# The start of a two-block transformer stack in split float32: another order of loads, splits, squares and norm sums in the first stage

## The chip, the cores and the metric

The kernel runs on one core of one Trainium2 chip. A core has a matmul engine (TensorE, PE in the profile), VectorE (DVE), ScalarE (ACT), GpSimd (POOL) and SyncE (SP), which issues most DMAs. Each engine works through its own instructions in order, and semaphores tie them together. The metric is the device time of one execution in microseconds (us); less is better.

## The reference, cut to what matters

Two blocks run one after the other on a sequence of 256 tokens plus 16 meta tokens, 272 columns in all, with 1024 features. Each block has two layers. A layer of the first block is a feed-forward part (ffn), a mixer and a second ffn:

```python
for l in range(DEPTH):
    h = h + 0.5 * swiglu(rms_norm(h, ffn1_norm[l]), ffn1_w_gu[l], ffn1_w_down[l])
    u = rms_norm(h, mix_norm[l])
    ...
    h = h + merged @ w_out[l]
    h = h + 0.5 * swiglu(rms_norm(h, ffn2_norm[l]), ffn2_w_gu[l], ffn2_w_down[l])
```

`rms_norm(h, w)` is h times w, divided by the root of the mean of h squared over the features; `swiglu` is silu(x W_gate) times x W_up, times W_down. The second block also adds a table of relative-position bias (`rel_bias`) to its attention scores. All of it is float32.

## The kernel before

The activations h lie transposed, as 8 tiles (k = 0 to 7) of 128 features by 272 tokens. A product of the matmul engine takes operands that were rounded, so every float32 operand is split in two: a high part, made by ScalarE (`x_hi` for h times the gain, L868; `split_hi` for weights, L858), and a low part, the rest, made by VectorE (`x_lo`, L1212; `split_lo`, L1201). Each product is then three matmuls: low weight by high input, high weight by low input, high by high. A weight chunk `raw[k]` holds the 8 feature tiles (1024 columns) that make one output tile; four chunks stand in a ring and are called a quad.

The first ffn of the first layer is the stage that the change is about. Its quad 0 is `raw[0]` to `raw[3]`. The first two output tiles (0 and 1) run as a group in `first_tiles` (L546 to L548): for every feature tile i, the three matmuls of chunk 0 and then those of chunk 1, 48 matmuls in all. Then come tiles 2 to 7, one by one, 24 matmuls each, in `k8_tile` (L513 to L515), and then a loop over quads. Tile 4 is the first one of quad 1, tile 8 the first one of quad 2.

The division by the root is put off. GpSimd squares the 8 tiles of h and adds them up in `acc` (one squaring, then seven pairs of a squaring L1795 and an addition L1798), TensorE sums `acc` over the features with a matrix of ones (`norm_sum`, L522), ScalarE takes the root (`std`, L862), VectorE the reciprocal (`rstd`, L1206), and VectorE multiplies each finished tile by it as it reads it out (`z`). In this stage the sum stands on TensorE between tiles 1 and 2. On ScalarE and VectorE the splits of quad 1 stand ahead of the root and the reciprocal (`first_splits`); each may start when the tile that used its place in the ring is done.

Before the stage the program does some small things: SyncE loads the one-hot bucket rows and the bias table (semaphore `rel_in`), the vectors with all gains (`vec`), h in two halves, four weight chunks, the constants and the masks. TensorE makes the bias rows with one product (`brow`, L827), ScalarE copies them (L1150), SyncE writes them to memory (`rows`). VectorE works out two small coefficient vectors (`lb`, `lam`, L1642 to L1684) in 24 instructions on 4 or 8 columns, with ScalarE's Exp and Ln between them (L1162 to L1167), and casts the masks (L1686). These stand behind the splits of quad 0 and ahead of those of quad 1, on both engines. The order on every engine is the order in which the code is written.

Of the kernel before, what the change touches and what calls it, by code (L numbers as in the profile page):

```python
# [43 lines left out]
RING = 4  # L44
# [178 lines left out]
def program(nc, a):  # L223
    with ExitStack() as ctx:
# [106 lines left out]
        NORM = 7  # L331
# [105 lines left out]
        def _(sp):  # L437
            def load(src, q, k, cols):

                if not isinstance(q, int) or q >= 1:  # L440
                    sp.wait_ge(lo_made, (q - 1) * RING + k + 1)
                sp.dma_start(raw[:, k, 0:cols], src).then_inc(landed[k], 16)
# [8 lines left out]
                stream(a["ffn_gu"], f * 2 * KF, q, FFN_GU_QUADS, CH8)  # L451
                stream(a["ffn_down"], f * 2 * KD, q + FFN_GU_QUADS, FFN_DOWN_QUADS, CH11)

            sp.dma_start(onehot[0:N_BUCKETS + 1, :], a["bucket_rows"]).then_inc(rel_in, 16)
            sp.dma_start(relt[0:N_BUCKETS + 1, :], a["rel_rows"]).then_inc(rel_in, 16)
            sp.dma_start(vec[:, :], a["vectors"]).then_inc(vec_in, 16)
            for s in range(2):
                sp.dma_start(h[:, 4 * s:4 * s + 4, :], a["h0"][:, 4 * s:4 * s + 4, :]).then_inc(h_in[s], 16)
            for k in range(2):
                load(a["ffn_gu"][k], 0, k, CH8)  # L460
            sp.dma_start(consts[:, :], a["consts"]).then_inc(consts_in, 16)
            for k in range(2, RING):
                load(a["ffn_gu"][k], 0, k, CH8)
            sp.dma_start(gate_flat, a["masks"]).then_inc(masks_in, 16)
            sp.wait_ge(brow_made, 1)
            sp.dma_start(rows[:, :], brow[0:HEADS, :]).then_inc(rows_out, 16)
            stream(a["ffn_gu"], RING, 1, FFN_GU_QUADS - 1, CH8)
            stream(a["ffn_down"], 0, FFN_GU_QUADS, FFN_DOWN_QUADS, CH11)
            sp.wait_ge(rows_out, 16)
            stream(a["mix"], 0, FFN_QUADS, MIX_QUADS - HEADS, CH8)  # L470
# [34 lines left out]
        def _(pe):  # L505
# [32 lines left out]
            def first_tiles(q, group, src, c, ready, norm=None):  # L538


                hi, lo = src
                at_c = c if t_wide(hi) else 0

                def products(k, i):
                    out, w = bank[k][:, 0:T - c], slice(i * P, i * P + P)
                    pe.matmul(out, wlo[:, k, w], hi[:, i, at_c:], start=(i == 0), stop=False)  # L546
                    pe.matmul(out, whi[:, k, w], lo[:, i, at_c:], start=False, stop=False)  # L547
                    return pe.matmul(out, whi[:, k, w], hi[:, i, at_c:], start=False, stop=(i == 7))  # L548

                for k in range(group):  # L550
                    pe.wait_ge(lo_made, q * RING + k + 1)
                for i in range(6):
                    ready(i)
                    for k in range(group):
                        products(k, i)
                for k in range(group):
                    for i in (6, 7):
                        if k == 0:
                            ready(i)
                        mm = products(k, i)  # L560
                    mm.then_inc(tile_done, 1)
                    if norm and k == (0 if group == RING else group - 1):
                        norm()
# [12 lines left out]

            def ffn(q, j, x, n, f, c, main_norm=True):
                group = RING if c else 2
                first_tiles(q, group, (xhi, xlo), c, inputs_ready(x), input_norm(x, n, c) if main_norm else None)
                for t in range(group, 2 * RING):  # L580
                    k8_tile(q + t // RING, t % RING, j + 4 if t == 7 else None, early_bank(t), (xhi, xlo), c)
                with pe.Fori(2, FFN_GU_QUADS) as b:
                    for k in range(RING):
                        k8_tile(b + q, k, b * RING + j + k - 3, k, (xhi, xlo), c)
# [234 lines left out]
            def scores2(hd):  # L819
                if hd >= 2:  # L820
# [3 lines left out]
                          stop=True).then_inc(s2_done, 1)  # L824

            pe.wait_ge(rel_in, 32)
            pe.matmul(bank[6][0:HEADS, :], relt[0:N_BUCKETS + 1, :], onehot[0:N_BUCKETS + 1, :],  # L827
                      start=True, stop=True).then_inc(brow_done, 1)
            pe.wait_ge(consts_in, 16)
            pe.wait_ge(brow_made, 1)  # L830
            with pe.Fori(0, DEPTH) as l:
                ffn(**layer_stage(l, 0))
# [19 lines left out]
        def _(act):  # L852
# [263 lines left out]
            def attention():  # L1116
# [29 lines left out]
                norm_std(n + 1, c)  # L1146
                inputs_from_h(13, 12, c)

            act.wait_ge(brow_done, 1)
            act.activation(brow[0:HEADS, :], bank[6][0:HEADS, :], ACT.Copy).then_inc(brow_made, 1)  # L1150
            act.wait_ge(vec_in, 16)
            for k in range(KD):
                if k % 4 == 0:
                    act.wait_ge(h_in[k // 4], 16)
                x_hi(0, k, 0)
            for k in range(RING):
                split_hi(0, k, CH8, 0)
            act.wait_ge(consts_in, 16)
            act.activation(warm[:, :], eps, ACT.Copy)
# [37 lines left out]
        def _(dve):  # L1197
# [437 lines left out]
            for k in range(KD):  # L1635
                if k % 4 == 0:
                    dve.wait_ge(h_in[k // 4], 16)
                x_lo(0, k, 0)
            for k in range(RING):
                split_lo(0, k, CH8)  # L1640
            r0, r1 = vec[:, VEC["lb_raw"]:VEC["lb_raw"] + 4], vec[:, VEC["lb_raw"] + 4:VEC["lb_raw"] + 8]
            dve.tensor_tensor(lb[:, 3, 0:4], r0, r1, ALU.max)  # L1642
# [79 lines left out]
        def _(pool):  # L1722
# [66 lines left out]
            def of_layer(st):  # L1789
                squares_of(h, 0, st["n"] + 1, lambda k: pool.wait_ge(tile_read, st["j"] + 2 * KF + k + 1))  # L1790

            for k in range(KD):
                if k % 4 == 0:
                    pool.wait_ge(h_in[k // 4], 16)
                pool.tensor_tensor((sqt[:, k % 2, :] if k else acc[:, :]), h[:, k, :], h[:, k, :], ALU.mult)  # L1795
                pool.drain()
                if k:
                    op = pool.tensor_tensor(acc[:, :], acc[:, :], sqt[:, k % 2, :], ALU.add)  # L1798
# [124 lines left out]
```

## Time and profile before

| | us |
|---|---|
| median of 3 runs | 2566.45 |
| lowest and highest | 2561.85 and 2567.02 |
| the profiled execution | 2565.33 |
| its span | 2563.5 |
| TensorE busy | 2357.3 (92%) |
| VectorE busy | 1553.2 (61%) |
| ScalarE busy | 1146.8 (45%) |
| GpSimd busy | 693.1 (27%) |

The span runs from the first instruction to the last, and the profiled execution has 1.8 us outside it. TensorE is busy nearly everywhere, so a stretch in which it waits costs its length, and work on another engine costs nothing as long as TensorE doesn't come to wait for it. The mean clock that TensorE was granted is 0.952 of full speed.

### The profile page before, as it was taken

To read this page: it belongs to the slowest core of one execution; us is meant where nothing else is said; L and a number is where in the kernel's file an instruction comes from. 1 tells how busy PE (TensorE), PEld (TensorE's weight loads), DVE (VectorE), ACT (ScalarE), POOL (GpSimd) and SP (SyncE) were. 2 spreads that over 40 slices of the span, in tenths; PEclk is the share of its full clock that TensorE was granted. 3 is DMA by queue.
4 is the path that set the end of the run, shared out by engine and by line. 5 is a ranking of instruction groups with operands and counts; after the bars stand their busy time and mean duration, and the time that the engine had idled before them with its cause. 6 is when DMAs were issued, how large, how long until landed. Compare 5 with 4: busy or idle time off the path is not lost.

```text
span 2563.5 us, 50134 instructions
## 1 busy us (share of the span) xinstructions
PE 2357.3 (92%) x18052; PEld 2269.9 (89%) x18052; DVE 1553.2 (61%) x2043; ACT 1146.8 (45%) x1620; POOL 693.1 (27%) x737
## 2 busy tenths in 40 slices
PE   7999988899999999879999999976899899977997
PEld 7999875799999998856899999976799899966997
DVE  6556775465545557853655575587665755575654
ACT  5445542344444446432454345355453445343542
POOL 4321220133213211300332142234532222224321
PEclk9999997999999999887999999988899999988999
DMA  5554331255545544221455445533355455531552
GB/s 205 180 177 160 107 120 66 75 167 182 180 133 189 185 146 137 99 83 41 139 174 197 140 164 194 175 115 115 134 191 193 151 185 188 182 107 66 197 193 102
DMA packets 99326, 380.12 MB, mean 148 GB/s; under 512 B 10975, under 2 KB 13151, under 8 KB 99208
## 3 DMA queue, kind: packets, MB, share of 16 engines
q1 hardware_dynamic: 99208, 378.56, 43.6%
q8 instruction: 72, 1.18, 0.2%
q14 instruction: 46, 0.38, 0.0%
HBM read 377.46 MB, written 3.16 MB: 148 GB/s over the span
## 4 chain that ended last, share of the span: by engine, by line
PE 52%; issue 32%; POOL 6%; DVE 5%; POOLq 2%; ACT 2%; DVEq 1%; DMA 0%; ACTq 0%; SPq 0%
PE bank L513 16%; PE bank L515 16%; PE bank L514 16%; POOL acc L1731 2%; POOL kd L1777 2%; POOLq L1729 2%; PE bank L546 1%; PE bank L547 1%; PE bank L548 1%; DVE h L1503 1%; DVE wlo L1201 1%; DVE xlo L1212 1%; DVE rstd L1206 1%; POOL midlo L1785 1%; ACT whi L858 1%
## 5 line engine op out<-in xcount | busy, mean ns | idle before, releaser
L1201 DVE TENSOR_TENSOR wlo<-raw,whi 128x1024 fp32r<-128x1024 f32 (+1 forms) x660 | 897.3, 1370 | 418.3 <-ACT whi L858 417.3
L858 ACT ACTIVATE whi<-raw 128x1024 fp32r<-128x1024 f32 (+1 forms) x660 | 727.7, 1116 | 627.9 <-PE bank L515 586.2
L513 PE MATMUL bank<-xhi,wlo 128*128 128x272 f32 (+1 forms) x3344 | 967.5, 289 | 5.9 <-DVE wlo L1201 3.4
L515 PE MATMUL bank<-xhi,whi 128*128 128x272 f32 (+1 forms) x3344 | 962.5, 288 | 0.0
L514 PE MATMUL bank<-xlo,whi 128*128 128x272 f32 (+1 forms) x3344 | 960.5, 287 | 0.0
L513 PEld LDWEIGHTS bank<-xhi,wlo 128*128 128x128 f32 x3344 | 638.1, 191 | 8.6 <-issue 4.8
L515 PEld LDWEIGHTS bank<-xhi,whi 128*128 128x128 f32 x3344 | 637.6, 191 | 0.0
L514 PEld LDWEIGHTS bank<-xlo,whi 128*128 128x128 f32 x3344 | 636.5, 190 | 0.2
L515 PE MATMUL bank<-hidhi,whi 128*128 128x272 f32 (+1 forms) x1408 | 401.7, 285 | 0.0
L513 PE MATMUL bank<-hidhi,wlo 128*128 128x272 f32 (+1 forms) x1408 | 400.4, 284 | 0.0
L514 PE MATMUL bank<-hidlo,whi 128*128 128x272 f32 (+1 forms) x1408 | 399.9, 284 | 0.0
L1748 POOL TENSOR_TENSOR z<-sil,z 128x272 f32<-128x272 f32 (+1 forms) x176 | 172.5, 980 | 604.9 <-DVE z L1238 454.8
L513 PEld LDWEIGHTS bank<-hidhi,wlo 128*128 128x128 f32 x1408 | 265.5, 189 | 0.0
L514 PEld LDWEIGHTS bank<-hidlo,whi 128*128 128x128 f32 x1408 | 265.0, 188 | 0.0
L515 PEld LDWEIGHTS bank<-hidhi,whi 128*128 128x128 f32 x1408 | 264.7, 188 | 0.0
L1752 POOL TENSOR_TENSOR hidlo<-z,hidhi 128x272 f32 (+1 forms) x176 | 165.9, 942 | 131.0 <-ACT hidhi L898 131.0
L868 ACT ACTIVATE xhi<-h,vec 128x256 fp32r<-128x256 f32 (+2 forms) x104 | 52.5, 515 | 269.6 <-DVE h L1256 177.3
L898 ACT ACTIVATE hidhi<-z 128x272 f32 (+3 forms) x176 | 74.9, 425 | 151.6 <-POOL z L1748 151.6
L546 PE MATMUL bank<-xhi,wlo 128*128 128x256 f32 (+1 forms) x288 | 92.0, 319 | 46.2 <-DVE xlo L1212 29.2
L1728 POOL TENSOR_TENSOR sqt<-h 128x272 f32<-128x272 f32 (+1 forms) x84 | 59.9, 713 | 227.8 <-DVE h L1256 191.3
L1731 POOL TENSOR_TENSOR acc<-acc,sqt 128x256 f32<-128x256 f32 (+1 forms) x126 | 116.0, 921 | 17.9
L1231 DVE TENSOR_TENSOR z<-bank,rstd 128x272 f32<-128x272 f32 (+1 forms) x176 | 75.8, 431 | 72.7 <-PE bank L515 71.4
(296 smaller groups left out, 2847.2 us busy)
## 6 DMA issues: line engine op xcount, KB each, us to landing
raw<-ffn_gu SPq DMA_DIRECT2D x352, 512.0 KB, 3.3
raw<-ffn_down SPq DMA_DIRECT2D x128, 704.0 KB, 4.1
raw<-mix SPq DMA_DIRECT2D x120, 512.0 KB, 3.3
raw<-rec SPq DMA_DIRECT2D x28, 512.0 KB, 3.5
raw<-kv SPq DMA_DIRECT2D x16, 512.0 KB, 4.2
raw<-att SPq DMA_DIRECT2D x16, 512.0 KB, 4.3
bias_rows<-rows SPq DMA_DIRECT2D x8, 256.0 KB, 4.6
bias<-bias_rows SPq DMA_DIRECT2D x1, 1536.0 KB, 8.6
```

The lines of the kernel that those rows point to most:

```text
L513: pe.matmul(out, wlo[:, slot, w], xh(i), start=(i == 0), stop=False)
L514: pe.matmul(out, whi[:, slot, w], xl(i), start=False, stop=False)
L515: mm = pe.matmul(out, whi[:, slot, w], xh(i), start=False, stop=(i == last))
L546: pe.matmul(out, wlo[:, k, w], hi[:, i, at_c:], start=(i == 0), stop=False)
L858: act.activation(whi[:, k, 0:cols], raw[:, k, 0:cols], ACT.Copy).then_inc(hi_made, 1)
L898: act.activation(hidhi[:, at_i, c:T], z[:, 2 + p:3 + p, c:T], ACT.Copy).then_inc(hid_hi_made, 1)
L1201: dve.tensor_tensor(wlo[:, k, 0:cols], raw[:, k, 0:cols], whi[:, k, 0:cols].bitcast(F32), ALU.subtract).then_inc(lo_made, 1)
L1231: dve.tensor_tensor(z[:, p, c:T], bank[banks[2 * p]][:, 0:T - c], rstd[:, c:T], ALU.mult).then_inc(tile_read, 1)
L1728: pool.tensor_tensor((sqt[:, k % 2, c:T] if k else acc[:, c:T]), src[:, k, c:T], src[:, k, c:T], ALU.mult)
L1731: op = pool.tensor_tensor(acc[:, c:T], acc[:, c:T], sqt[:, k % 2, c:T], ALU.add)
L1748: pool.tensor_tensor(z[:, 2 + p, c:T], sil[:, p, c:T], z[:, 2 + p, c:T], ALU.mult).then_inc(hid_made, 1)
L1752: pool.tensor_tensor(hidlo[:, at_i, c:T], z[:, 2 + p:3 + p, c:T], hidhi[:, at_i, c:T].bitcast(F32), ALU.subtract).then_inc(hid_lo_made, 1)
```

## The change

On SyncE, the bucket rows, the bias table and the vectors are gone from the head of the queue. The halves of h and weight chunks 0 and 1 come first, in turns, then chunks 2 and 3, the constants and the masks. The write of the bias rows, and the wait for them, comes after the whole stream of the gate and up weights. ScalarE issues the three small loads at its own head, the vectors first.

On ScalarE and VectorE the splits of weight chunks 0 and 1 stand behind those of h tiles 0 and 1; those of chunks 2 and 3 stay behind all of h. GpSimd starts its squares of h only when all 8 low tiles of h are made. TensorE waits for a chunk's low part at that chunk's first product, not for both chunks ahead of all products, and for the constants at the norm sum. In each ffn of the two layers (4 executions) the norm sum stands behind tile 3, no longer behind tile 1. The bias product goes to another PSUM bank.

```diff
-            sp.dma_start(onehot[0:N_BUCKETS + 1, :], a["bucket_rows"]).then_inc(rel_in, 16)
-            sp.dma_start(relt[0:N_BUCKETS + 1, :], a["rel_rows"]).then_inc(rel_in, 16)
-            sp.dma_start(vec[:, :], a["vectors"]).then_inc(vec_in, 16)
             for s in range(2):
                 sp.dma_start(h[:, 4 * s:4 * s + 4, :], a["h0"][:, 4 * s:4 * s + 4, :]).then_inc(h_in[s], 16)
-            for k in range(2):
+                load(a["ffn_gu"][s], 0, s, CH8)
+            for k in range(2, RING):
                 load(a["ffn_gu"][k], 0, k, CH8)
             sp.dma_start(consts[:, :], a["consts"]).then_inc(consts_in, 16)
-            for k in range(2, RING):
-                load(a["ffn_gu"][k], 0, k, CH8)
             sp.dma_start(gate_flat, a["masks"]).then_inc(masks_in, 16)
+            stream(a["ffn_gu"], RING, 1, FFN_GU_QUADS - 1, CH8)
             sp.wait_ge(brow_made, 1)
             sp.dma_start(rows[:, :], brow[0:HEADS, :]).then_inc(rows_out, 16)
-            stream(a["ffn_gu"], RING, 1, FFN_GU_QUADS - 1, CH8)
...
-                for k in range(group):
-                    pe.wait_ge(lo_made, q * RING + k + 1)
                 for i in range(6):
                     ready(i)
                     for k in range(group):
+                        if i == 0:
+                            pe.wait_ge(lo_made, q * RING + k + 1)
                         products(k, i)
...
-                first_tiles(q, group, (xhi, xlo), c, inputs_ready(x), input_norm(x, n, c) if main_norm else None)
+                first_tiles(q, group, (xhi, xlo), c, inputs_ready(x), input_norm(x, n, c) if c and main_norm else None)
                 for t in range(group, 2 * RING):
                     k8_tile(q + t // RING, t % RING, j + 4 if t == 7 else None, early_bank(t), (xhi, xlo), c)
+                    if c == 0 and t == 3:
+                        pe.wait_ge(consts_in, 16)
+                        input_norm(x, n, c)()
...
-            pe.matmul(bank[6][0:HEADS, :], relt[0:N_BUCKETS + 1, :], onehot[0:N_BUCKETS + 1, :],
+            pe.matmul(bank[NORM][0:HEADS, :], relt[0:N_BUCKETS + 1, :], onehot[0:N_BUCKETS + 1, :],
                       start=True, stop=True).then_inc(brow_done, 1)
-            pe.wait_ge(consts_in, 16)
...
+            act.dma_start(vec[:, :], a["vectors"]).then_inc(vec_in, 16)
+            act.dma_start(onehot[0:N_BUCKETS + 1, :], a["bucket_rows"]).then_inc(rel_in, 16)
+            act.dma_start(relt[0:N_BUCKETS + 1, :], a["rel_rows"]).then_inc(rel_in, 16)
             act.wait_ge(brow_done, 1)
...
                 x_hi(0, k, 0)
-            for k in range(RING):
+                if k < 2:
+                    split_hi(0, k, CH8, 0)
+            for k in range(2, RING):
                 split_hi(0, k, CH8, 0)
...
                 x_lo(0, k, 0)
-            for k in range(RING):
+                if k < 2:
+                    split_lo(0, k, CH8)
+            for k in range(2, RING):
                 split_lo(0, k, CH8)
...
+            pool.wait_ge(h_in[0], 16)
+            pool.wait_ge(h_in[1], 16)
+            pool.wait_ge(x_lo_made, 8)
             for k in range(KD):
-                if k % 4 == 0:
-                    pool.wait_ge(h_in[k // 4], 16)
                 pool.tensor_tensor((sqt[:, k % 2, :] if k else acc[:, :]), h[:, k, :], h[:, k, :], ALU.mult)
```

The first instructions of ScalarE, before. `brow` is the bias rows, `xhi` and `whi` the high parts of h and of the weights:

```order
L1150 ACT_TABLE_LOAD
L1150 ACTIVATE brow<-bank 8x512 [waits brow_done]
L868 ACTIVATE xhi<-h,vec 128x272 [waits h_in0,vec_in]
L868 ACTIVATE xhi<-h,vec 128x272 x3
L868 ACTIVATE xhi<-h,vec 128x272 [waits h_in1]
L868 ACTIVATE xhi<-h,vec 128x272 x3
L858 ACTIVATE whi<-raw 128x1024 [waits landed0]
L858 ACTIVATE whi<-raw 128x1024 [waits landed1]
```

The same place of the changed kernel:

```order
L1147 DMA vec<-vectors 128x268
L1148 DMA onehot<-bucket_rows 33x512
L1149 DMA relt<-rel_rows 33x8
L1151 ACT_TABLE_LOAD
L1151 ACTIVATE brow<-bank 8x512 [waits brow_done]
L866 ACTIVATE xhi<-h,vec 128x272 [waits h_in0,vec_in]
L856 ACTIVATE whi<-raw 128x1024 [waits landed0]
L866 ACTIVATE xhi<-h,vec 128x272
L856 ACTIVATE whi<-raw 128x1024 [waits landed1]
L866 ACTIVATE xhi<-h,vec 128x272 x2
```

The copy of the bias rows, with its wait, still stands ahead of all splits; the first weight split moved from behind eight splits of h to behind one, and three loads stand at the head.

TensorE from the end of tile 1 to the start of tile 2, before; `acc` is the sum of squares:

```order
L547 MATMUL bank<-xlo,whi 128x272
L548 MATMUL bank<-xhi,whi 128x272
L521 REGISTER_ALU
L522 MATMUL bank<-acc,consts 128x272 [waits sq_made]
L527 REGISTER_ALU
L513 MATMUL bank<-xhi,wlo 128x272 [waits lo_made]
```

The changed kernel from the end of tile 3 to the start of tile 4:

```order
L510 MATMUL bank<-xlo,whi 128x272
L511 MATMUL bank<-xhi,whi 128x272
L517 REGISTER_ALU [waits consts_in]
L518 MATMUL bank<-acc,consts 128x272 [waits sq_made]
L523 ISA
L509 MATMUL bank<-xhi,wlo 128x272 [waits lo_made]
```

The sum moved two tiles back, and the wait for the constants moved to it; behind it now stands the first tile of quad 1.

## Rows read from the trace of the kernel before

**Rows 1.** Timeline: start us, us, engine, line, op, out<-in, xcount [idle <-releaser].
```profile
1.26 0.31 SPq L455 DMA_DIRECT2D relt<-rel_rows  x1
...
2.01 0.90 SPq L458 DMA_DIRECT2D h<-h  x2
...
3.00 1.87 PE L827 MATMUL bank<-onehot,relt 33*8 33x512 f32 x2 [3.00 <-DMA relt<-rel_rows]
...
4.92 0.59 ACT L1150 ACTIVATE brow<-bank 8x512 f32<-8x512 f32 x1 [2.89 <-PE bank L827]
...
6.09 3.40 ACT L868 ACTIVATE xhi<-h,vec 128x272 fp32r<-128x272 f32 x8 [0.59 <-DMA h<-h]
...
9.41 1.99 ACT L858 ACTIVATE whi<-raw 128x1024 fp32r<-128x1024 f32 x2
...
16.60 0.59 PE L546 MATMUL bank<-xhi,wlo 128*128 128x272 f32 x1 [11.73 <-DVE wlo L1201]
```
**Rows 2.** DMA issues, first 60 us: KB each, median us from issue to landing.
```profile
gate<-masks SPq DMA_DIRECT2D x1, 512.0 KB, 10.0
```
**Rows 3.** Durations by line: ns min/median/max, first and last start us.
```profile
L1212 DVE SCALAR_TENSOR_TENSOR xlo<-h,vec,xhi x8: 501/502/1124, 518.7 to 542.1; 128x272 fp32r<-128x272 f32 x8
L1201 DVE TENSOR_TENSOR wlo<-raw,whi x4: 1656/1716/1779, 13.1 to 18.1; 128x1024 fp32r<-128x1024 f32 x4
L1201 DVE TENSOR_TENSOR wlo<-raw,whi x8: 1215/1220/1227, 27.7 to 48.3; 128x1024 fp32r<-128x1024 f32 x8
```
**Rows 4.** Timeline of PE, the same columns: the sum, then tiles 4 and 8.
```profile
24.70 0.62 PE L522 MATMUL bank<-acc,consts 128*128 128x272 f32 x2
...
31.20 0.29 PE L513 MATMUL bank<-xhi,wlo 128*128 128x272 f32 x1
...
43.31 0.37 PE L513 MATMUL bank<-xhi,wlo 128*128 128x272 f32 x1
```
**Rows 5.** Windows: us, PE busy (xmatmuls), PEld, DVE, ACT, POOL, PEclk, DMA, GB/s.
```profile
16.60:20.85 4.25, 4.25 (x19) 4.25 (x20) 4.18 (x4) 0.00 (x0) 4.11 (x4) 1.00 0.85 281
20.85:24.60 3.75, 3.75 (x31) 3.75 (x31) 2.24 (x14) 1.19 (x3) 0.88 (x2) 1.00 0.59 212
```
**Rows 6.** Timeline of POOL: squarings and additions.
```profile
18.80 1.57 POOL L1798 TENSOR_TENSOR acc<-acc,sqt 128x272 f32<-128x272 f32 x1
20.33 0.64 POOL L1795 TENSOR_TENSOR sqt<-h 128x272 f32<-128x272 f32 x1
21.11 0.77 POOL L1798 TENSOR_TENSOR acc<-acc,sqt 128x272 f32<-128x272 f32 x1
```
**Rows 7.** Timeline of DVE and ACT, 19 to 42 us.
```profile
19.66 0.72 DVE L1642 TENSOR_TENSOR lb<-vec 128x4 f32<-128x4 f32 x1
20.46 0.52 DVE L1644 TENSOR_TENSOR lb<-vec,lb 128x4 f32<-128x4 f32 x1
...
23.61 0.21 ACT L1165 ACTIVATE lam<-lam 128x8 f32<-128x8 f32 x1 [2.31 <-DVE lam L1665]
...
25.44 0.17 DVE L1672 TENSOR_SCALAR lb<-lam 128x8 f32<-128x8 f32 x1 [1.34 <-ACT lam L1167]
...
26.65 2.96 ACT L858 ACTIVATE whi<-raw 128x1024 fp32r<-128x1024 f32 x3
...
32.48 1.28 ACT L862 ACT_TABLE_LOAD   x1
...
41.88 1.22 DVE L1201 TENSOR_TENSOR wlo<-raw,whi 128x1024 fp32r<-128x1024 f32 x1 [3.71 <-ACT whi L858]
```
**Rows 8.** Windows of two later stretches, the columns of rows 5.
```profile
741.90:747.90 6.00, 6.00 (x26) 6.00 (x27) 1.08 (x1) 1.28 (x1) 0.00 (x0) 0.50 0.54 182
...
339.00:341.70 2.70, 2.69 (x12) 2.70 (x13) 1.48 (x3) 2.70 (x4) 1.59 (x2) 0.50 0.00 0
```
**Rows 9.** Timeline of PE: the idle time ahead of those two stretches.
```profile
339.01 0.55 PE L742 MATMUL bank<-qd,kd 128*128 128x128 f32 x1 [4.14 <-DVE dec L1407]
...
741.90 0.59 PE L546 MATMUL bank<-xhi,wlo 128*128 128x272 f32 x1 [3.54 <-DVE wlo L1201]
```

More of the change, by code:

```diff
@@ L1147, in attention @@
                 inputs_from_h(13, 12, c)
+            act.dma_start(vec[:, :], a["vectors"]).then_inc(vec_in, 16)
+            act.dma_start(onehot[0:N_BUCKETS + 1, :], a["bucket_rows"]).then_inc(rel_in, 16)
+            act.dma_start(relt[0:N_BUCKETS + 1, :], a["rel_rows"]).then_inc(rel_in, 16)
             act.wait_ge(brow_done, 1)
-            act.activation(brow[0:HEADS, :], bank[6][0:HEADS, :], ACT.Copy).then_inc(brow_made, 1)
+            act.activation(brow[0:HEADS, :], bank[NORM][0:HEADS, :], ACT.Copy).then_inc(brow_made, 1)
             act.wait_ge(vec_in, 16)
```

## The prediction

> **What bounds the kernel now.** TensorE is busy 92% of the span, so I read the timeline of its first wait. Its first real product starts at 16.60, after 11.73 us of idle time that VectorE's low weights ended [rows 1]. I follow that wait back. VectorE made 8 low tiles of h and then 2 low chunks; ScalarE made 8 high tiles from 6.09 and the chunks only at 9.41, 1.99 us for two; and ahead of them stand the copy of the bias rows, from 4.92, and the product it copies, from 3.00 [rows 1]. From 16.60 on TensorE does not stop: the 48 products of tiles 0 and 1 end when the norm sum starts at 24.70, tile 4 starts at 31.20 and tile 8 at 43.31 [rows 4]. What counts is how much earlier tiles 4 and 8 start; behind tile 8 the stage runs on matmuls alone and a shift passes through whole.
>
> **Start of the splits: nothing gained.** h is issued 1.25 us earlier (three issues between 0.76 and 2.01 are gone), but ScalarE still copies the bias rows first. The table was issued at 1.26 and its product started at 3.00, 1.74 later. Now it is ScalarE's third issue, at about 1.66: landing at 3.4 if alone. Beside the stream of h and weights it shares the transfer engines; no row shows a load from ScalarE's queue. Lower bound 3.4; upper bound the masks' 10.0 us from issue to landing [rows 2], so 11.7. The bias rows had nothing of size ahead of them and now have little in their own queue, so I take 4.2. Product and copy follow as before: from 3.00 to ScalarE free at 5.51 are 2.5, so 6.7, and the first high tile starts at 6.85, against 6.09 before.
>
> The Trainium skill (DMA: Bandwidth & Descriptors, Queues, rings and completion order) says that SyncE's and ScalarE's loads run in separate rings on the same 16 transfer engines, which take packets from them in turns. By that rule the small loads are not held behind the megabytes of SyncE's ring, which is the near end of my range.
>
> **The alternating splits: 5.8 us.** High tile 0 ends at 7.3, high chunk 0 (1.0) at 8.3, high tile 1 at 8.7. Chunk 1 was the last of the bytes that ScalarE found there at 10.4 (second of the two from 9.41); issued 1.25 earlier it is there by 8.7. High chunk 1 ends at 9.7, tiles 2 to 7 at 12.2 (0.41 each, 3.40 by 8), chunks 2 and 3 at 14.1. VectorE, with GpSimd held back, needs 0.50 for a low tile and 1.22 for a low chunk instead of 1.72 [rows 3]: low chunk 0 at 9.6, low chunk 1 at 11.1, low tile 7 at 13.7. TensorE does three products at 9.6, waits, and runs from 11.2. The first 19 matmuls took 4.25 us (0.224 each: the 1.2 GHz level, though the clock column has no record before 20.85 and says 1.00), the next 31 took 3.75 (0.121, the 2.4 GHz level) [rows 5]. With the same 4.25 us before the rise, the remaining 45 take 4.25 + 26 by 0.126 = 7.55. The group ends at 18.8, not 24.6: 5.8 us, and the feed of one low tile per 0.5 us keeps up.
>
> **GpSimd's squares: they now end last.** They start at 13.8, no longer when h lands. Beside nothing big, a squaring and an addition take 1.55 (20.33 to 21.88); beside VectorE's low chunks each operation takes 1.6, double [rows 6]. One squaring at 0.78 and seven pairs are 11.6; low chunks 2 and 3 (13.7 to 17.0) cost two operations their double time, 1.7. End: 27.1; bounds 25.4 (no contention) and 28.7 (two chunks of quad 1 fall in as well). TensorE, done with tiles 2 and 3 (6.05 us, since 31.20 less the sum's 0.45 and its start at 24.70) at 24.8, waits for the sum until 27.2.
>
> **VectorE's small work: now beside GpSimd.** Behind low chunk 3 (17.0, against 19.66) stand the 24 small instructions. While GpSimd worked, one on 4 columns took 0.72 and 0.52; alone 0.17 at 25.44 [rows 7]. The longer ones end within 0.02 us of GpSimd's operation [rows 6]. Before, only the first few met GpSimd; now nearly all do. From 19.66 to ScalarE's second Exp at 23.61 were 3.95 us, nine steps that wait for each other. At one step per GpSimd operation (0.78) they are 7.0; at the old pace 3.9. In the pause between two operations one more step slips in, so I take 5.6: Exp at 22.6. From there ScalarE's Ln and table loads take 3.05 until the first high chunk of quad 1 (26.65) [rows 7]: 25.65. VectorE's own rest began at 25.44 and was done when ScalarE's first split (1.0 from 26.65) was, so it takes at most 2.3 alone; half of it beside GpSimd, it ends with the cast about 28.1, and low chunk 0 of quad 1 is there at 29.3. Bounds: 27.0 with no contention on the small steps, 30.5 with one step per operation.
>
> The Trainium skill (SBUF — State Buffer, two separate sides) calls the port pair of VectorE and GpSimd an exclusive lock that an operation holds for its whole length, the other blocking. By that rule the upper bound, 30.5, would hold; the rows agree with it as far as 0.52 and 0.72 go.
>
> **The sum for tile 4.** It starts at 29.3 instead of 31.2: 1.9 us gained of 5.8, bounds 4.2 and 0.7. The other 3.9 are new idle time of TensorE, 24.8 to 29.3 with the sum in it.
>
> **Price of the idle time.** After a pause of 4.14 us the granted clock was 0.50 for another 2.7 us, after one of 3.54 for 6.0 [rows 8, 9]. At half speed half of that is lost: 1.35 to 3.0; I take 2.3. Tile 8 then starts at 29.3 + 12.1 + 2.3 = 43.7 against 43.31. Is something else late there? From the sum's table load on ScalarE (32.48) to the low chunk that tile 8 needs (41.88 + 1.22) are 10.6 us [rows 7]. ScalarE's four splits of quad 1 now end at 29.7, VectorE's low ones at about 33.5, 1.5 later than its reciprocal wants to start: 41.9, hidden by 1.8.
>
> **The small parts.** The sum behind tile 3 in the other three ffns of the layers: TensorE never waits for it there, and tile 3 is done 0.25 earlier; ScalarE's split of it takes 1.06, so the sum is ready in time. A wait of 0.1 at tile 8 may go: 0 to 0.3 gained. Waits per chunk: at most the three matmuls of one chunk per group, and only where the weights end the wait; elsewhere the splits of h or a loop's return do: 0. SyncE's write of the bias rows, behind the stream, is needed only by the mixer: 0. The second load ring starts earlier, at low chunk 0 (9.6 against 15.06), since SyncE passes no wait; the masks were issued before it: no cost.
>
> Total: 0.4 lost, 0.15 gained, so +0.25. The profiled execution took 2565.33, which becomes 2565.6; it lies 1.1 under the median of 2566.45, where the same sum gives 2566.7. The three runs are 5.2 us apart. I forecast 2566.5.
>
> **The rivals.**
> (a) The gain is kept whole: the squares end before 24.8 and the small steps don't meet them. Against it: seven pairs at 1.55 from 13.8 alone end at 25.4. Then tile 4 starts at 25 to 26, no fall of the clock: 5.2 to 6.4 gained, about 2560.5.
> (b) Half is kept: the small steps run at the old pace (27.0), the pause is 2 us and the clock falls briefly or not: 4.2 less 0 to 1.35, about 2563.
> (c) Slower: the bias table, third in ScalarE's queue, lands late, and its copy holds ScalarE and with it every split. At a landing of 4.2 ScalarE reaches chunk 1 just as it lands (6.85 + 1.85 = 8.7), so each us past 4.2 moves everything by one. It decides past 0.2% (5.1 us) from a landing at 9.1; at the masks' pace, 11.7, it costs 7.5: 2574. Against it: its queue holds only the vectors and the bucket rows ahead of it, where the masks had h, four chunks and the constants.
> (d) Steps one per GpSimd operation and a long fall of the clock: tile 4 at 30.5, 3.0 lost: +2.3, about 2568.5.
>
> The skill's lock rule is (d); I give it the chance that two matching rows of early steps bear out.
>
> **How the numbers follow.** Forecast 0.44, (a) 0.10, (b) 0.17, (c) 0.07, (d) 0.22. The likeliest is the forecast: 2566.5. Measurements of this kernel tell about 0.2%, 5.1 us, from no change. Faster by more: (a) and a little of (b), 0.13; slower by more: (c) and a little of (d), 0.11; within: 0.76. The range 2561.5 to 2571.5 leaves out (a) and (c) and holds the spread of the runs around the rest.
>
> **What would show it.** After: first high tile of h near 6.9; TensorE's long run from 11.2; the group done at 18.8; GpSimd's first squaring at 13.8 and last addition at 27; small VectorE steps of 0.5 to 0.7 us through it; the sum near 27.2, tile 4 at 29.3, clock 0.50 behind it, tile 8 near 43.7. Wrong if the clock stays up through the pause, if the squares end before tile 3, or if the bias product starts past 4.5.

## The result

The changed kernel takes 2568.76 us (median of 20 runs, 2564.71 to 2573.43); the kernel before, measured beside it, takes 2564.67 (2559.16 to 2567.31). The ratio is 1.0015, with a 95% interval of 1.0008 to 1.0022: 3.8 us slower, 2.1 to 5.6. It is slower, and by less than the 0.2% at which the prediction drew its line. The profiled execution took 2571.45 us, its span is 2569.4.

What answers to [rows 1] in the changed kernel, from the timeline of its start: start us, us, engine, line, operation, operands, count, and in brackets the idle time before and what ended it.

```profile
0.75 0.42 ACTq L1147 DMA_DIRECT2D vec<-vectors  x1
1.20 0.64 ACTq L1148 DMA_DIRECT2D onehot<-bucket_rows  x1
1.87 0.30 ACTq L1149 DMA_DIRECT2D relt<-rel_rows  x1
...
8.03 1.87 PE L826 MATMUL bank<-onehot,relt 33*8 33x512 f32 x2 [8.03 <-DMA relt<-rel_rows]
...
9.94 0.59 ACT L1151 ACTIVATE brow<-bank 8x512 f32<-8x512 f32 x1 [6.45 <-PE bank L826]
10.43 0.50 ACT L866 ACTIVATE xhi<-h,vec 128x272 fp32r<-128x272 f32 x1
...
13.20 0.60 PE L542 MATMUL bank<-xhi,wlo 128*128 128x272 f32 x1 [3.29 <-DVE wlo L1204]
```

The product of the bias table starts at 8.03, not at 3.00. It was issued at 1.87 and is used 6.2 us later; before it was 1.7. ScalarE stands behind it until 9.94, and the first high tile of h starts at 10.43, not at 6.09. Even so TensorE's first product comes 3.4 us earlier than before, at 13.20: the alternating splits work. Then GpSimd and VectorE, 17 to 31 us:

```profile
17.34 2.61 POOL L1801 TENSOR_TENSOR acc<-h 128x272 f32<-128x272 f32 x1 [16.89 <-DVE xlo L1215]
...
22.38 0.77 POOL L1804 TENSOR_TENSOR acc<-acc,sqt 128x272 f32<-128x272 f32 x1
...
29.94 0.76 POOL L1804 TENSOR_TENSOR acc<-acc,sqt 128x272 f32<-128x272 f32 x1
...
17.08 2.35 DVE L1204 TENSOR_TENSOR wlo<-raw,whi 128x1024 fp32r<-128x1024 f32 x2
...
22.41 0.77 DVE L1659 TENSOR_TENSOR lb<-lb 128x4 f32<-128x4 f32 x1
...
28.47 0.75 DVE L1684 TENSOR_TENSOR lam<-lam,lb 128x8 f32<-128x8 f32 x1
...
29.98 1.27 DVE L1691 CAST masks<-gate 128x1024 uint8<-128x1024 f32 x1
```

The squares end at 30.70, where they ended at 21.88. Small steps of 4 or 8 columns take up to 0.77 us, against 0.17 alone [rows 7], and the cast takes 1.27, against 0.69 in the kernel before. And TensorE, timeline and then windows (us, TensorE busy and its matmuls, weight loads, VectorE, ScalarE, GpSimd, granted clock, DMA share, GB/s):

```profile
30.75 0.73 PE L518 MATMUL bank<-acc,consts 128*128 128x272 f32 x2 [2.19 <-POOL acc L1804]
...
32.44 0.51 PE L509 MATMUL bank<-xhi,wlo 128*128 128x272 f32 x1 [0.96 <-DVE wlo L1204]
...
46.16 0.29 PE L509 MATMUL bank<-xhi,wlo 128*128 128x272 f32 x1
```

```profile
32.50:36.00 3.50, 3.50 (x16) 3.50 (x17) 3.50 (x4) 2.83 (x3) 0.00 (x0) 0.51 0.71 209
36.00:46.10 10.10, 10.10 (x82) 10.10 (x82) 6.21 (x10) 3.83 (x7) 4.23 (x5) 1.00 0.41 144
```

TensorE is done with tile 3 and waits 2.19 us for the squares, makes the sum, and waits 0.96 for low chunk 0 of quad 1. Tile 4 starts at 32.44, 1.2 us later than in [rows 4]. Behind the pause the granted clock is 0.51, the 1.2 GHz level, for 3.5 us: from tile 4 to tile 8 are 13.72 us, where they were 12.11, so it costs 1.6. Tile 8 starts at 46.16, against 43.31: 2.85 us later. The gain of 3.4 us at the first product is 2.35 at the end of tiles 0 and 1 (22.35), and has turned into a loss within 33 us.

### The profile page after: what moved, and what is told of

Its sections match the earlier page's. It is cut to its first block, busy times and chain, and to the rows that moved or that the text cites. A ratio compares the mean times of both kernels' runs of the same rounds, so it can differ in the third digit from the quotient of the medians.

```text
span 2569.4 us, 50128 instructions
## 1 busy us (share of the span) xinstructions
PE 2366.6 (92%) x18052; PEld 2273.6 (88%) x18052; DVE 1551.3 (60%) x2043; ACT 1146.6 (45%) x1620; POOL 690.0 (27%) x737
## 4 chain that ended last, share of the span: by engine, by line
PE 50%; issue 32%; POOL 6%; DVE 6%; POOLq 2%; ACT 2%; DVEq 2%; DMA 0%; ACTq 0%
PE bank L509 16%; PE bank L511 15%; PE bank L510 15%; POOL acc L1736 2%; POOL kd L1782 2%; POOLq L1734 2%; DVE h L1506 1%; DVE wlo L1204 1%; PE bank L542 1%; DVE xlo L1215 1%; DVE rstd L1209 1%; POOL midlo L1790 1%; PE bank L543 1%; PE bank L544 1%; ACT whi L856 1%
```

## The experiments

All positions are read from the timelines, each from one profiled execution. "Tile 8" is the first matmul of quad 2; from there on the first stage runs on TensorE alone in all of these kernels.

**The late bias table, undone.** Only the bucket rows and the bias table go back to the head of SyncE's queue.

```diff
-            act.dma_start(onehot[0:N_BUCKETS + 1, :], a["bucket_rows"]).then_inc(rel_in, 16)
-            act.dma_start(relt[0:N_BUCKETS + 1, :], a["rel_rows"]).then_inc(rel_in, 16)
+            sp.dma_start(onehot[0:N_BUCKETS + 1, :], a["bucket_rows"]).then_inc(rel_in, 16)
+            sp.dma_start(relt[0:N_BUCKETS + 1, :], a["rel_rows"]).then_inc(rel_in, 16)
```

> The changed kernel, but the bucket rows and the bias table are loaded by SyncE ahead of h again; the vectors stay on ScalarE's queue. Theory A (the late bias table holds ScalarE, and every split behind it moves one for one): bias product at 3.0 instead of 8.0, ScalarE reaches h near 6.3, high chunk 1 done near 10.6 instead of 13.2 because its landing then bounds it; everything 2.6 us earlier: tiles 0 and 1 done near 19.7, tile 4 at 29.8, tile 8 near 43.5, ratio to before about 1.000. Rival B (the squares and the clock's fall decide, not the table): tile 4 stays at 32 or later and the ratio stays near 1.0015.

Tile 8 at 44.03, ratio 1.0009 (1.0000 to 1.0018). Its timeline:

```profile
3.57 1.87 PE L828 MATMUL bank<-onehot,relt 33*8 33x512 f32 x2 [3.57 <-DMA relt<-rel_rows]
...
6.27 0.52 ACT L868 ACTIVATE xhi<-h,vec 128x272 fp32r<-128x272 f32 x1 [0.20 <-DMA h<-h]
7.74 1.06 ACT L858 ACTIVATE whi<-raw 128x1024 fp32r<-128x1024 f32 x1 [0.95 <-DMA raw<-ffn_gu]
8.71 0.51 ACT L868 ACTIVATE xhi<-h,vec 128x272 fp32r<-128x272 f32 x1
10.38 1.06 ACT L858 ACTIVATE whi<-raw 128x1024 fp32r<-128x1024 f32 x1 [1.17 <-DMA raw<-ffn_gu]
```

The table lands in time, ScalarE starts 4.2 us earlier, and then waits 0.95 and 1.17 us for the two weight chunks, so that high chunk 1 ends 1.8 us earlier, not 2.6. Tile 4 (30.44) and tile 8 move by 2.0 and 2.1. For the positions theory A holds, a little smaller than it said (tile 4 at 29.8, tile 8 at 43.5), and B falls; the times of the two kernels are too close to tell.

**The loads alone.** The kernel before with the three loads on ScalarE's queue, nothing else.

```diff
-            sp.dma_start(onehot[0:N_BUCKETS + 1, :], a["bucket_rows"]).then_inc(rel_in, 16)
-            sp.dma_start(relt[0:N_BUCKETS + 1, :], a["rel_rows"]).then_inc(rel_in, 16)
-            sp.dma_start(vec[:, :], a["vectors"]).then_inc(vec_in, 16)
...
+            act.dma_start(vec[:, :], a["vectors"]).then_inc(vec_in, 16)
+            act.dma_start(onehot[0:N_BUCKETS + 1, :], a["bucket_rows"]).then_inc(rel_in, 16)
+            act.dma_start(relt[0:N_BUCKETS + 1, :], a["rel_rows"]).then_inc(rel_in, 16)
             act.wait_ge(brow_done, 1)
```

> The kernel before, with one part of the change alone: vectors, bucket rows and bias table are loaded from ScalarE's queue. Theory A: the bias product starts near 8, the copy ends near 10.5, the first high tile starts 4.3 us later than before; the squares of GpSimd go on undisturbed meanwhile, so VectorE's low tiles and chunks meet fewer of them and part comes back: first long run of TensorE near 18, tile 4 near 32.5, tile 8 near 44.6, +1.3 us, ratio 1.0005. If the lateness costs all it holds, tile 8 is at 47.6 and the ratio is 1.0017. Rival B: no loss, below 0.5 us.

Tile 8 at 47.39, 4.1 us later and not 1.3; ratio 1.0008 (0.9999 to 1.0017). The bias product starts at 8.16, the first high tile 4.5 us later than before, TensorE's first product 3.6 (20.17); the other 0.5 comes from the clock, which rose 5.6 us behind that product, where the profile of before has 4.5. GpSimd's squares, from 5.34 to 17.46, still cover nearly all 8 low tiles of VectorE, since these came later too:

```profile
11.21 6.55 DVE L1212 SCALAR_TENSOR_TENSOR xlo<-h,vec,xhi 128x272 fp32r<-128x272 f32 x8 [11.21 <-ACT xhi L865]
17.69 4.62 DVE L1201 TENSOR_TENSOR wlo<-raw,whi 128x1024 fp32r<-128x1024 f32 x4
```

0.82 us for a low tile, against 0.80 before; only the chunks were spared (1.16 each, against 1.66).

**The sum alone.** The kernel before with the norm sum behind tile 3 in the ffns of the layers.

```diff
-                first_tiles(q, group, (xhi, xlo), c, inputs_ready(x), input_norm(x, n, c) if main_norm else None)
+                first_tiles(q, group, (xhi, xlo), c, inputs_ready(x), input_norm(x, n, c) if c and main_norm else None)
...
+                    if c == 0 and t == 3:
+                        input_norm(x, n, c)()
```

> The kernel before, with one part of the change alone: in the ffns of the layers the norm sum stands behind tile 3 instead of tile 1. Both theories: nobody waits for it, tile 3 is done 0.25 us earlier, tile 8 starts 0 to 0.1 earlier in each of the four stages; ratio 1.000 within 0.0005, and no new pause of TensorE.

Ratio 0.9998 (0.9989 to 1.0008). No new pause: the sum follows tile 3 at once.

```profile
31.43 0.29 PE L515 MATMUL bank<-xhi,whi 128*128 128x272 f32 x1
31.55 0.62 PE L522 MATMUL bank<-acc,consts 128*128 128x272 f32 x2
31.81 0.49 PE L513 MATMUL bank<-xhi,wlo 128*128 128x272 f32 x1
```

Tile 8 is at 44.11 in this execution, but its first product was already 0.35 us late (16.95), and the spacing of the products puts the rise to full speed 5.4 us behind it, not 4.5 as in the profile of before, which costs 0.45. Both come before anything that the edit moved, and together they are the 0.8.

**The squares, undone.** The changed kernel, GpSimd starting when h lands.

```diff
-            pool.wait_ge(h_in[0], 16)
-            pool.wait_ge(h_in[1], 16)
-            pool.wait_ge(x_lo_made, 8)
             for k in range(KD):
+                if k % 4 == 0:
+                    pool.wait_ge(h_in[k // 4], 16)
```

> The changed kernel, but GpSimd starts its squares when h lands, as before. Theory A: squares from 5.5 to about 19, while ScalarE still waits for the bias table; no pause at the sum; low chunks and tiles of VectorE somewhat slower, but the small steps of VectorE run alone after 20.5 and take 4 us to the second Exp instead of 6; tile 4 near 29.8 instead of 32.4, no fall of the clock there, tile 8 near 42.0 against 46.1 of the changed kernel and 43.3 before; ratio near 0.9995. Rival B (the late table alone makes the loss): tile 4 stays near 32.

Tile 4 at 30.30, tile 8 at 42.65, ratio 0.9993 (0.9984 to 1.0002). The squares end at 18.95. The small steps behind them are fast again:

```profile
22.27 0.15 DVE L1647 TENSOR_TENSOR lb<-vec 128x4 f32<-128x4 f32 x1
...
24.88 0.21 ACT L1168 ACTIVATE lam<-lam 128x8 f32<-128x8 f32 x1 [1.91 <-DVE lam L1670]
```

From the end of low chunk 3 (22.35) to the second Exp they take 2.5 us; in the changed kernel, beside the squares, 5.9 (19.43 to 25.32). TensorE waits 0.7 us at tile 4 and its clock stays up. Theory A holds: with the table late, holding the squares back cost 3.5 us at tile 8, 2.1 of them at tile 4 and the rest in the clock.

**Both undone.**

```diff
-            pool.wait_ge(x_lo_made, 8)
...
-            act.dma_start(onehot[0:N_BUCKETS + 1, :], a["bucket_rows"]).then_inc(rel_in, 16)
-            act.dma_start(relt[0:N_BUCKETS + 1, :], a["rel_rows"]).then_inc(rel_in, 16)
+            sp.dma_start(onehot[0:N_BUCKETS + 1, :], a["bucket_rows"]).then_inc(rel_in, 16)
+            sp.dma_start(relt[0:N_BUCKETS + 1, :], a["rel_rows"]).then_inc(rel_in, 16)
```

> The changed kernel with two parts undone: bucket rows and bias table ahead of h on SyncE, and GpSimd's squares from h's landing. If the late table (2.1 us at tile 8 in the run with it undone) and the held-back squares (3.5 us in the run with that undone) are two causes that add up: tile 4 near 28.2, tile 8 near 40.5, against 46.16 of the changed kernel and 43.31 before; ratio 0.9987. If they are one cause seen twice: tile 8 near 42.5.

Tile 8 at 42.65, where the squares undone alone gave 42.65; ratio 1.0007 (0.9997 to 1.0016). They don't add up. VectorE, from its timeline:

```profile
13.80 5.24 DVE L1215 SCALAR_TENSOR_TENSOR xlo<-h,vec,xhi 128x272 fp32r<-128x272 f32 x6
18.97 3.37 DVE L1204 TENSOR_TENSOR wlo<-raw,whi 128x1024 fp32r<-128x1024 f32 x2
22.26 0.15 DVE L1647 TENSOR_TENSOR lb<-vec 128x4 f32<-128x4 f32 x1
```

VectorE starts its low parts 3.9 us earlier, but now all of them fall beside the squares (6.22 to 21.25): six low tiles take 5.24 us where they took 4.34 with the table late, two chunks 3.37 instead of 2.35. That is half of the 3.9. The other half goes to ScalarE's waits for the two weight chunks, 1.97 and 1.13 us; they landed 1.0 later than in the run with the table undone, whose loads are the same, so landings differ by as much from one execution to the next. VectorE reaches the small steps at 22.26, where it reached them at 22.27 with the table late. That tie is a coincidence of sizes; tile 4 waits for VectorE's chain in both, so the earlier start of the splits was worth nothing here, where it was worth 2.0 us at tile 4 with the squares held back.

The four kernels together, tile 8 against before: neither undone +2.9, table undone +0.7, squares undone -0.7, both undone -0.7. So the late table costs 2.1 us only beside held-back squares, and the held-back squares cost 3.5 us with the table late and 1.4 with it in time.

**The small steps, moved.** The changed kernel with VectorE's `lb` block ahead of the first low tile and its `lam` block between `ffn(**F4)` and `ffn_down(**F4)`, ScalarE's Exp and Ln with them.

```diff
             dve.wait_ge(vec_in, 16)
+            r0, r1 = vec[:, VEC["lb_raw"]:VEC["lb_raw"] + 4], vec[:, VEC["lb_raw"] + 4:VEC["lb_raw"] + 8]
+            dve.tensor_tensor(lb[:, 3, 0:4], r0, r1, ALU.max)
...
             ffn(**F4)
+            raw_lam = vec[:, VEC["lam"]:VEC["lam"] + KD]
...
             ffn_down(**F4)
```

> The changed kernel, but VectorE's and ScalarE's small steps are gone from between the splits of quads 0 and 1: those for lb stand ahead of the first low tile, where VectorE waits for h anyway, those for lam between the gate and up tiles and the down tiles of the fifth ffn. Theory A (the held-back squares and the small steps beside them each end at nearly the same time): low chunk 0 of quad 1 is there near 25 instead of 32.4, but the squares then run beside low chunks again and end near 32, so tile 4 starts at 31.5 to 33 and little is gained. Rival C (the small steps alone decide tile 4): tile 4 near 29.5.

Tile 4 at 35.77, later than expected and 3.3 us later than in the changed kernel; ratio 1.0032 (1.0019 to 1.0044), the slowest of all. Low chunk 0 of quad 1 is there at 23.89, as expected. The squares pay for it:

```profile
22.94 1.57 POOL L1802 TENSOR_TENSOR acc<-acc,sqt 128x272 f32<-128x272 f32 x1
24.48 1.62 POOL L1799 TENSOR_TENSOR sqt<-h 128x272 f32<-128x272 f32 x1
...
34.27 0.76 POOL L1802 TENSOR_TENSOR acc<-acc,sqt 128x272 f32<-128x272 f32 x1
...
35.08 1.27 PE L518 MATMUL bank<-acc,consts 128*128 128x272 f32 x2 [6.79 <-POOL acc L1802]
```

They run beside four low chunks of quad 1 and end at 35.03. Rival C falls: the small steps are not what decides the changed kernel alone. With them out of the way the squares, slowed by the low chunks, are what ends last. I had put the end of the squares at 32: the first squaring took 3.19 us, and four later ones 1.6 to 1.7.

**All three.** The table and the squares as before, the small steps moved.

```diff
...
+            sp.dma_start(relt[0:N_BUCKETS + 1, :], a["rel_rows"]).then_inc(rel_in, 16)
...
-            pool.wait_ge(x_lo_made, 8)
...
             dve.wait_ge(vec_in, 16)
+            r0, r1 = vec[:, VEC["lb_raw"]:VEC["lb_raw"] + 4], vec[:, VEC["lb_raw"] + 4:VEC["lb_raw"] + 8]
...
             ffn(**F4)
+            raw_lam = vec[:, VEC["lam"]:VEC["lam"] + KD]
```

> All three together: bucket rows and bias table ahead of h on SyncE, squares from h's landing, small steps moved as described for the run with them alone moved. Theory A: nothing is late for tile 4 but TensorE itself; tiles 0 and 1 done near 20.5, tile 4 near 27.0, tile 8 near 39.2, no fall of the clock before 250 us, ratio 0.9984. If moving the small steps costs time in the fifth ffn, that stage is longer than before by as much.

Tile 4 at 26.75, tile 8 at 39.60; ratio 0.9992 (0.9983 to 1.0002). TensorE no longer waits in front of tile 4. It waits 0.39 us at tile 8, though: ScalarE's last split of quad 1 waited until 27.73 for its weight chunk to land. The fifth ffn shows no loss: over the same stretch (1450 to 1712 us before, 1441.5 to 1703.5 here) TensorE waits 19.8 us, against 21.3.

**Chunk 1 ahead of the second half of h**, on top of that:

```diff
-            for s in range(2):
-                sp.dma_start(h[:, 4 * s:4 * s + 4, :], a["h0"][:, 4 * s:4 * s + 4, :]).then_inc(h_in[s], 16)
-                load(a["ffn_gu"][s], 0, s, CH8)
+            sp.dma_start(h[:, 0:4, :], a["h0"][:, 0:4, :]).then_inc(h_in[0], 16)
+            load(a["ffn_gu"][0], 0, 0, CH8)
+            load(a["ffn_gu"][1], 0, 1, CH8)
+            sp.dma_start(h[:, 4:8, :], a["h0"][:, 4:8, :]).then_inc(h_in[1], 16)
```

> As the run with all three together, and weight chunk 1 is loaded ahead of the second half of h. The landing of chunk 1 bounded the alternating splits there (ScalarE waited 1.2 us for it in the run with the table undone): high chunk 1 about 1.2 us earlier, tile 8 near 38.2, ratio 0.9980. If the second half of h is late instead, ScalarE waits at its fifth high tile.

Tile 8 at 38.53; ratio 0.9988 (0.9979 to 0.9998). ScalarE no longer waits for chunk 1, nor for the second half of h. Tile 4 starts at 26.22, 0.5 us earlier; the other 0.5 at tile 8 is the wait of 0.39 there, which this execution doesn't have. The same kernel again:

> The same kernel as the run with all three together and chunk 1 ahead of the second half of h, again, for the time: tile 8 at 38.5, ratio to before 0.9988 within 0.0008. If the gain was a draw of the clock's falls, the ratio is 1.000.

Ratio 0.9985 (0.9975 to 0.9995), tile 4 at 26.22 again, tile 8 at 38.92, with the wait (0.23) back. This version beats the kernel before by 3 to 4 us, and so the changed one by about 7 (an estimate: both were measured against before, not against each other).

**The late table alone**, in that kernel:

```diff
-            sp.dma_start(onehot[0:N_BUCKETS + 1, :], a["bucket_rows"]).then_inc(rel_in, 16)
-            sp.dma_start(relt[0:N_BUCKETS + 1, :], a["rel_rows"]).then_inc(rel_in, 16)
...
+            act.dma_start(onehot[0:N_BUCKETS + 1, :], a["bucket_rows"]).then_inc(rel_in, 16)
+            act.dma_start(relt[0:N_BUCKETS + 1, :], a["rel_rows"]).then_inc(rel_in, 16)
```

> The kernel of the run before this one in the same call, and only the bucket rows and the bias table go through ScalarE's queue, as in the change. Nothing else is late there, so the whole price of the late table shows: bias product at 7.9 instead of 3.6, first high tile of h at 10.3 instead of 6.2, less what the squares do meanwhile without meeting VectorE; tile 4 near 29.2 instead of 26.2, tile 8 near 41.5 instead of 38.5, ratio to before 0.9993. If the table's lateness is mostly hidden, as it was between the two runs with the squares at h's landing (both at 42.66), tile 8 stays under 39.5.

Tile 8 at 42.14, 3.2 us behind its pair (38.92); ratio 0.9994 (0.9985 to 1.0004). The bias product is 3.9 us later (7.45 against 3.56), the first high tile 3.3 (9.85 against 6.56). But not all of the 3.2 is the table's. TensorE's run without a wait, which begins with the second chunk's first product, starts 2.4 later, at 15.11 against 12.72, and the clock then rose 6.0 us into it, against 3.3. Here first, the pair second, up to the rise:

```profile
15.11:21.14 6.03, 6.03 (x26) 6.03 (x27) 6.03 (x8) 3.29 (x5) 3.73 (x5) 1.00 0.35 122
12.72:16.03 3.31, 3.31 (x15) 3.31 (x15) 3.31 (x4) 2.11 (x4) 3.03 (x5) 1.00 1.02 411
```

Both stretches have 0.22 to 0.23 us per product, the 1.2 GHz level (the clock column has no record yet and says 1.00). The later rise makes 1.2 of the 3.6 us by which tiles 0 and 1 end later, and the pair loses 0.4 at tile 8. In the changed kernel, with the table late too, the rise came after 4.2 us, with the squares undone after 2.9; so the late table isn't shown to delay it. What the table is worth in this kernel is then about 2.4 us, an estimate from the two starts. In the changed kernel 4.5 us of lateness cost 2.1 and ScalarE's waits for the chunks took most of the rest; with the squares at h's landing the price was 0.

**TensorE kept busy ahead of the weights.**

```diff
+            for _ in range(3):
+                pe.matmul(bank[6][0:HEADS, :], relt[0:N_BUCKETS + 1, :], onehot[0:N_BUCKETS + 1, :],
+                          start=True, stop=True)
```

> As the best kernel, and TensorE repeats the bias product three times into a spare bank, work that nothing reads, so that it is busy from 3.6 until the first weights are there. If the clock rises on that work: granted clock 1.00 before 10 us, the first products 0.125 us apart, tiles 0 and 1 then bound by VectorE's low parts (low chunk 3 at 20.8), done near 19.2 instead of 19.9, tile 8 near 37.9. If the clock does not rise on it, or the last repetition delays the first product past 9.9: tile 8 at 38.5 or later.

```profile
3.53 1.87 PE L829 MATMUL bank<-onehot,relt 33*8 33x512 f32 x2 [3.53 <-DMA relt<-rel_rows]
5.19 5.32 PE L832 MATMUL bank<-onehot,relt 33*8 33x512 f32 x6
10.45 0.59 PE L545 MATMUL bank<-xhi,wlo 128*128 128x272 f32 x1
...
12.94 0.59 PE L545 MATMUL bank<-xhi,wlo 128*128 128x272 f32 x1 [1.45 <-DVE wlo L1207]
13.33 0.43 PE L546 MATMUL bank<-xlo,whi 128*128 128x272 f32 x1
13.56 0.43 PE L547 MATMUL bank<-xhi,whi 128*128 128x272 f32 x1
```

TensorE was busy without a gap from 3.53 to past 10.4, and the products behind it still stand 0.227 us apart, the 1.2 GHz level, until 16.48. In the same kernel without that work they do so until 16.03. So the clock rose no earlier for it. Tile 8 is at 39.33, no earlier. Yet the ratio is 0.9973 (0.9962 to 0.9985, 6 runs), below that of the same kernel without it, with intervals that overlap. No place in the trace accounts for it; it stays open.

**The runs together.** Tile 8 against before, and the time against before (the ratio less 1, times 2565 us), all in us; the interval of the time is 1.7 either way for the changed kernel and 2.3 to 3.2 for the others:

| kernel | tile 8 | time |
|---|---|---|
| changed | +2.9 | +3.8 |
| table undone | +0.7 | +2.3 |
| loads alone | +4.1 | +2.1 |
| sum alone | +0.8 | -0.5 |
| squares undone | -0.7 | -1.8 |
| both undone | -0.7 | +1.8 |
| small steps moved | +6.1 | +8.2 |
| all three | -3.7 | -2.1 |
| and chunk 1 first | -4.8 | -3.1 |
| the same again | -4.4 | -3.8 |
| and table late | -1.2 | -1.5 |
| and TensorE kept busy | -4.0 | -6.9 |

In each of the twelve the shift of tile 8 lies within the interval of the time. So no second cause behind tile 8 is needed for the 3.8 us, and none can be excluded below about 2 us: executions of one kernel lie up to 14 us apart, and the clock's later falls come at other places in each profile. The two profiles show it. Read at VectorE's reciprocals, the changed kernel is 2.8 us behind at 226 us, 7.9 at 554, 4.1 at 1285 and 5.9 at 2552. Between 226 and 554 all kernels built from the changed one lose, by 2.5 to 5.1 us against the profile of before, while the two built from the kernel before lose 0.9 and 1.3; up to 1285 all win back 0.7 to 7.8. TensorE's waits from 230 to 545 us are only 0.9 longer in the changed kernel, so most of it goes with the clock (granted 0.94 there from 230 to 285 us, 1.00 before). Whether something of the change acts there stays open.

## Why the prediction was right, and where it was not

The time lies in the range, and "no change beyond 0.2%" holds: the ratio is 1.0015. The forecast was a shift of +0.25 us, the measured one is +3.8 (2.1 to 5.6); tile 8 was forecast 0.4 later and came 2.85 later. So the range held with one term far off, and two things helped: it was 5 us wide on either side, and the kernel before came out at 2564.67 beside the changed one, 1.8 below the median from which the forecast was counted. One of the prediction's own signs of being wrong came true: the bias product started past 4.5.

**Start of the splits.** This is the term that was mis-sized. I took a landing of the bias table at 4.2, near the end of the range where it is alone; its product started at 8.03. ScalarE began at 10.43 instead of 6.85. The mechanism was written down as rival (c), ScalarE held by the copy of the bias rows; its size was a landing of 8, below the 9.1 from which it would have passed 0.2%. Putting the table back moved tile 8 by 2.1, to 44.03. That is the prediction's 43.7 within 0.3, but by two errors that cancel: tile 4 was 1.1 later than forecast (30.44 against 29.3), and the clock's fall behind it cost 0.8 less. Rival (c) had each us of lateness cost one, and 4.5 us cost 2.1. Here a second term was off, which the late table hid in the changed kernel: the landing of chunk 1, put at 8.7. With the table in time ScalarE waited for it until 10.38; about 0.9 of that is due to the two issues that stand at SyncE's head again.

What I argued, that the queue holds little of size ahead, missed what the table itself is: many tiny packets. The bytes per queue, from 2 to 5 us and from 5 to 8:

```profile
q1 hardware_dynamic: 182, 0.71, 63.0%
q10 hardware_dynamic: 188, 0.20, 20.3%
...
q1 hardware_dynamic: 323, 1.22, 101.5%
q10 hardware_dynamic: 44, 0.00, 0.8%
```

By 5 us ScalarE's queue (q10) had moved 0.20 of its 0.21 MB: the vectors and the bucket rows, the little of size. In the 3 us behind that, up to the bias product at 8.03, it moved 44 packets of next to no bytes, which fits the table's 33 rows of 32 bytes, while SyncE's queue (q1) moved 323 and 1.22 MB. The Trainium skill (DMA: Bandwidth & Descriptors, Queues, rings and completion order) says that the two queues are rings on the same 16 engines, served in turns; these lines agree with it, as both queues move packets in both stretches. The prediction took it to mean the near end of the range. My reading, which no run tests by itself, is that taking turns still holds each small packet behind large ones of the other queue: 6.2 us from issue to use.

**The alternating splits.** Right in kind and near in size: from the first high tile to the last of the group the prediction had 11.9 us (6.85 to 18.8), the trace has 11.9 (10.43 to 22.35). VectorE's low parts took 0.50 and 1.22 us without GpSimd, as written. The clock rose 4.2 us into the run without a wait, where I had taken the 4.25 of before; that was luck, as the runs above have 2.9 to 6.0.

**The squares.** Predicted 13.3 us from start to end (13.8 to 27.1), measured 13.4 (17.34 to 30.70), 2.0 of them from one squaring that met both low chunks (2.61 instead of 0.64) where I had two operations at double time, 1.7. TensorE waited for them, 2.19 us against 2.4.

**The small steps.** Predicted 5.6 us to the second Exp, beside the squares, and 3.9 at the old pace. Measured 5.9; alone 2.5. The bound of one step per GpSimd operation (7.0) was too slow: after a squaring there are 0.14 us before GpSimd's next operation, and a step slips in. The Trainium skill's lock rule (SBUF — State Buffer, two separate sides) was read to give that bound. That the long ones of the small steps end with GpSimd's operation, as the rule has it, the timeline shows (22.41 + 0.77 beside 22.38 + 0.77). Low chunk 0 of quad 1: predicted 15.6 us behind low tile 7 (13.7 to 29.3), measured 15.2 (17.2 to 32.4). That is closer than its parts: low chunks 2 and 3 took 2.35 us instead of 3.3, since GpSimd's first squaring gave way to them, and the steps up to the cast took 0.7 more.

**Pause and clock.** Both were forecast: a pause ahead of tile 4, a fall of the clock behind it. It cost 1.6 us where I took 2.3 between 1.35 and 3.0.

**The small parts.** The sum behind tile 3 costs nothing, as the run with it alone shows. Rivals (a) and (b), that the gain is kept, did not come; (d) had the right sign and nearly the time (2568.5), but not by its cause: the steps were faster than one per GpSimd operation, the fall of the clock cost 1.6 and not 3.0, and tile 4 came at 32.44, not 30.5, because the splits began 3.6 us later.

## What to carry to other kernels

Before a small load is moved to another queue, ask which engine waits for it in order: here a 1 KB table, whose rows are first fetched again at 326 us, stood ahead of every split, and its lateness was theirs. Where two engines slow each other down, moving one's work later only moved the meeting here; the gain came when work left the critical stretch (the small steps into idle time), and the same move can lose in one setting (1.0032, squares held back) and help in another (0.9985, with the table and the squares as before and chunk 1 first). Positions in the first 50 us told 2 us apart, where the times of a run of 2565 us did not; but read the clock's rise before a shift is put down to the edit, since it alone moved tile 8 by up to 1.2 us.

## What was not expected of the hardware

A 1 KB load, third on ScalarE's queue, took 6.2 us to be of use, while both queues together moved 409 GB/s from 5 to 8 us; at the head of SyncE's queue it took 1.7. GpSimd's first squaring took 2.61 us when it met two low chunks of VectorE that ran back to back at their own pace (1.2 each), while within a chain of squares both are slowed, in the kernel before an addition to 1.57 and a low chunk to 1.66 and more. The clock rose between 2.9 and 6.0 us into TensorE's first run without a wait, in the thirteen profiles of this case. And 7 us of TensorE work ahead of the weights, the bias product four times without a gap, did not bring the rise forward: it came at 16.48, and at 16.03 without that work.
